# Prompt attention: an order of its own for each engine, and queries turned from the projection's rows without a stage

## The chip, the cores and the metric

The kernel runs on one core of one Trainium2 chip. Its time is the device time of one execution in microseconds (us), the median of several runs. One core has TensorE (the matrix engine), VectorE, ScalarE, GpSimd and SyncE (which here issues DMAs). Each runs its own queue of instructions in order; they meet only at semaphores. In the profile they are PE (and PEld for its weight loads), DVE, ACT, POOL and SP.

## What is computed

One layer of a hybrid decoder, for a prompt of 1024 tokens and for 8 sequences of 8 new tokens. Cut to what matters here:

```python
p = in_proj(rmsnorm(x, norm_pre), w_in)          # q | k,v of three branches | gates | z | gla_* | conv_*
o_nsa = nsa(q, gates, kv_cmp, kv_slc, kv_win) * silu(z)   # 8 query heads x 64, 2 key heads
x = x + rmsnorm(concat(o_nsa, o_gla, o_conv) @ w_out, norm_post)

# nsa, for each block of 128 queries and each of the 4 query heads of a key head:
qs  = q * HEAD_DIM ** -0.5
o_c = softmax(qs @ k_compressed.T, mask) @ v_compressed   # one row per 64 tokens
o_s = softmax(qs @ k_selected.T, causal) @ v_selected     # 16 blocks of 64: for the prompt, all
o_w = softmax(qs @ k_window.T, last 512) @ v_window
o   = gate0 * o_c + gate1 * o_s + gate2 * o_w
```

## The kernel before

The kernel has three stages. `project` norms the input and makes most columns of the projection; `attend_prompt`, which the change rewrites in part, is the prompt's attention; `tail` holds the linear attention, the attention of the new tokens and the output projection. Values are kept nearly at full precision by splitting a tile into a rounded part (`hi`) and the remainder (`lo`), and multiplying both.

The attention works through 32 units: for each of 2 key heads, 8 blocks of 128 queries, each with a selected-branch unit (even numbers, all 1 to 8 key tiles up to the diagonal) and a window unit (odd numbers, at most 5 tiles). For each of a unit's 4 query heads there is a step "scores" (TensorE, line 1084, queries hi and lo against keys, into PSUM banks 0 to 3), a step "least" (VectorE's minimum, L1265) and a step "exp" (ScalarE, L1182). Then, key tile by key tile, "turn" transposes the probabilities of the four heads (TensorE, L1099, into bank 4 or 5), ScalarE copies them rounded (L1190) and VectorE makes the remainder (L1269); "sum" multiplies by the values (L1110, bank 6), and after the last tile ScalarE copies the sums (L1198). "output" turns them back (L1121) and VectorE scales and adds them (L1278 to L1291, tile `scaled`).

Once per block of queries and key head there are also: "query", which turns the queries (TensorE L1056, ScalarE L1170 to q_hi, VectorE L1244 to q_lo), "c_scores" (TensorE L1063 and VectorE L1251 to L1258), "c_exp" (ScalarE L1173, then six VectorE steps from L1298), "c_turn" (TensorE L1127, VectorE L1315) and "c_values" (TensorE L1131, VectorE L1318). These five and "output" share one bank, the spare bank 7: `spare()` makes TensorE wait until VectorE has read the use before. Before "query", VectorE writes the scaled queries twice side by side into the stage `q_st` (`stage_query`, L1207 and L1208), so that the transpose has them on both halves of the partitions; the keys lie there as hi on the first 64 and lo on the last 64.

At the start of each key head come "k_turn", "c_keys" (L1024), "c_rows" (L1031) and "v_stage": the keys and values of this head, turned, compressed and split.

Between all this stands the rest of the projection: 24 items ("rest", L1047) of 8 groups of three products, 192 groups, with the weights' split ("w_split", L1154 and L1234) and the results' way out ("rest_out", L1163, L1240). They use banks 1 and 3, which scores need as well once a unit has more than 4 tiles; so they can only run in the first half of each key head's blocks.

What sets the order: `schedule()` yields one list of steps, with fixed places for everything (`FILL` says how many rest groups go after each head of the first four blocks, `LAG` how far sums stand behind turns). TensorE, ScalarE, VectorE and SyncE all walk this same list, and each takes from it the steps in which it has a part. `place` numbers the uses of the spare bank in list order. `heads_before` and `items_before` find, for each user of banks 1 and 3, whom it has to wait for.

`tail` is ordered in another way: its own `schedule()` inside it is a planner. Each step is given its parts by engine with a duration, and `needs` names what each part waits for. The planner places the steps forward and then backward, and then forward again by the backward places, each engine for itself, and yields a list for each engine.

After the last rest product GpSimd makes the constants of `tail`, and SyncE issues its loads, among them 64 loads of pages (L1388) and the window (L1393).

Of the kernel before, what the change touches and what calls it, by code (L numbers as in the profile page):

```python
# [18 lines left out]
P = 128  # L19
D = 1024  # L20
KD = D // P
# [38 lines left out]
class Order:  # L60
# [19 lines left out]
    def wait(self):  # L80
        at = self.base + self.n
        self.eng.wait_ge(self.sem, at if self.it is None else self.it * self.per + at)

# [531 lines left out]
def attend_prompt(nc, sem, ident, pq, pk, pn, h_hi, h_lo, prob_win, s_cst, w_next, ps, L, z_dram, qk_dram, va_dram, gate_dram, w_in, w_cmp_k, w_cmp_v,  # L615
# [145 lines left out]

    def turn_bank(t):
        return 4 + t % 2
# [18 lines left out]
    with ExitStack() as ctx:  # L782
# [7 lines left out]
        q_st = sb("q_st", [P, NG, 2, HD])  # L790
# [39 lines left out]
        s_qst = sem("q_staged")  # L830
# [14 lines left out]
        with nc.Block() as block:  # L845
# [154 lines left out]
            def _(pe):  # L1000
# [6 lines left out]
                for what, x, y in steps:  # L1007
# [128 lines left out]
            def _(act):  # L1136
                for what, x, y in steps:
# [18 lines left out]
                    elif what == "rest_out":  # L1156
# [44 lines left out]
            def _(dve):  # L1201
                v = Order(dve, v_done)

                def stage_query(x):
                    kv, i = x // NT, x % NT
                    src = pq[:, i, kv * NG * HD:(kv + 1) * NG * HD].rearrange("p (g d) -> p g d", g=NG)
                    nc.vector.tensor_scalar(q_st[:, :, 0, :], src, -SCALE, None, ALU.mult)  # L1207
                    nc.vector.tensor_scalar(q_st[:, :, 1, :], src, -SCALE, None, ALU.mult).then_inc(s_qst, 1)  # L1208

                nc.vector.tensor_scalar(gate, gate, 0.5, 0.5, ALU.mult, ALU.add).then_inc(s_gate, 1)  # L1210
                for what, x, y in steps:
                    if what == "k_stage":
                        if x == 0:
                            stage_query(0)
                    elif what == "v_stage":
# [182 lines left out]
def tail(nc, sem, ident, pq, new, kc, ps, L, z_dram, qk_dram, va_dram, conv_dram, attn_dram, cache_slc_kv, cache_win_kv,  # L1398
# [384 lines left out]
    def sorted_by_need(keys, before):  # L1783
        out, seen = [], set()
        for key in keys:
            todo = [key]
            while todo:
                k = todo[-1]
                wait = [b for b, _ in before[k] if b not in seen]
                if wait:  # L1790
                    todo += wait
                else:
                    todo.pop()
                    if k not in seen:
                        seen.add(k)
                        out.append(k)
        return out

    def schedule():
        HANDOVER, WINDOW = 0.15, 0.3  # L1800
        ENGINES = "PE", "ACT", "DVE", "SP"
        lists = [list(decays()), list(linear()), list(sample_states()), [s for pi in range(PAIRS) for s in pair(pi)], list(project_out()),
                 list(gated(LASTM)), list(split_out())]
        heads, after, before = {}, {}, {}
        for n, steps in enumerate(lists):
            for step in steps:
                done = None
                for eng, cost in parts(step):
                    key = step, eng
                    line = heads.setdefault((n, eng), [])  # L1810
                    before[key] = [((s, e), lag + HANDOVER) for s, e, lag in needs(step, eng)]
                    if done:
                        before[key].append((done, HANDOVER))
                    if line:
                        before[key].append((line[-1][0], 0.0))
                    line.append((key, cost))
                    done = key
        cost = {key: c for line in heads.values() for key, c in line}
        for key in cost:
            for k, lag in before[key]:  # L1820
                after.setdefault(k, []).append((key, lag))

        def place(first, then, rank, window):
            missing = {key: len(first.get(key, [])) for key in cost}
            ready = dict.fromkeys(cost, 0.0)
            open_to = {eng: [key for key in cost if key[1] == eng and not missing[key]] for eng in ENGINES}
            free, at = dict.fromkeys(ENGINES, 0.0), {}
            while len(at) < len(cost):
                begin = lambda key: max(free[key[1]], ready[key])
                soonest, eng = min((min(map(begin, keys)), eng) for eng, keys in open_to.items() if keys)  # L1830
                key = min((key for key in open_to[eng] if begin(key) <= soonest + window), key=rank)
                open_to[eng].remove(key)
                at[key] = free[eng] = begin(key) + cost[key]
                for k, lag in then.get(key, []):
                    ready[k] = max(ready[k], at[key] + lag)
                    missing[k] -= 1
                    if not missing[k]:
                        open_to[k[1]].append(k)
            return at

        left = {}
        for key in reversed(sorted_by_need(cost, before)):
            left[key] = cost[key] + max([lag + left[a] for a, lag in after.get(key, [])], default=0.0)
        forward = place(before, after, lambda key: -left[key], 0.0)
        backward = place(after, before, lambda key: -forward[key], 0.0)
# [884 lines left out]
```

## Time and profile before

| | |
|---|---|
| median of 3 runs | 1014.05 us (1013.36 to 1018.79) |
| the profiled execution | 1020.7 us, of which the span from first to last instruction is 1019.0 us |
| TensorE busy | 935.7 us (92%) |
| VectorE busy | 595.0 us (58%) |
| ScalarE busy | 409.7 us (40%) |
| GpSimd busy | 190.9 us (19%) |
| `project` | about 0 to 285 us of the span |
| `attend_prompt` | about 285 to 720.5 us |
| `tail` | about 720.5 to 1019 us |

"Busy" is the time in which an engine executes; on TensorE the ends are modelled, so two products in a row overlap in the listing. PEclk is the granted clock of TensorE as a share of its full 2.4 GHz; it has two levels, full and half, so a clock of 0.9 over a stretch means a fifth of it at half. "A <- B" behind a wait means that A's engine sat idle until B's instruction released it.

### The profile page before, as it was taken

How to read it: one execution, taken by the hardware profiler on the slowest of the kernel's cores; microseconds unless marked ns; L12 is line 12 of the kernel's file. 1: busy time of each engine (PE TensorE's matmuls, PEld its weight loads, DVE VectorE, ACT ScalarE, POOL GpSimd, SP SyncE). 2: the span in 40 equal slices, each digit the busy share in tenths (PEclk: the TensorE clock that was granted, in tenths of full speed). 3: DMA queues.
4: the chain of work that ended last, by engine and by line, in shares of the span. 5: the costliest groups of instructions: out<-in, count | busy, mean ns of one | idle time of the engine just before them, and what ended most of it. 6: DMA issues, size and time to landing. Idle time of an engine off the chain costs nothing. (4 is left out here: it accounts for less than half of the span.)

```text
span 1019.0 us, 16705 instructions
## 1 busy us (share of the span) xinstructions
PE 935.7 (92%) x5935; PEld 808.9 (79%) x5935; DVE 595.0 (58%) x1428; ACT 409.7 (40%) x916; POOL 190.9 (19%) x178
## 2 busy tenths in 40 slices
PE   5999999998989988999999988999688999999997
PEld 5999999998979887777889867777445666777665
DVE  6531010194444576878555668787567867787653
ACT  6432111111023454666534445667264434434322
POOL 0049599999010000000000230000000000000000
PEclk9999999998999999999999979999688999999999
DMA  7127534534052101000011013300533455452321
GB/s 252 53 97 241 194 114 147 175 118 125 1 169 67 48 16 36 1 1 1 9 43 50 23 39 101 108 1 1 191 91 103 128 166 163 139 160 68 116 89 32
DMA packets 106820, 93.73 MB, mean 92 GB/s; under 512 B 21245, under 2 KB 99954, under 8 KB 104626
## 3 DMA queue, kind: packets, MB, share of 16 engines
q1 hardware_dynamic: 84946, 58.65, 19.1%
q10 hardware_dynamic: 19488, 17.25, 5.6%
q0 software_dynamic: 2304, 16.78, 4.8%
q8 instruction: 47, 0.77, 0.3%
q14 instruction: 35, 0.29, 0.1%
HBM read 78.16 MB, written 18.61 MB: 95 GB/s over the span
## 5 line engine op out<-in xcount | busy, mean ns | idle before, releaser
L592 PE MATMUL ps<-w_hi,h_hi 128*128 128x264 f32 (+5 forms) x432 | 123.9, 287 | 0.2 <-DVE h_lo L464 0.2
L592 PE MATMUL ps<-w_lo,h_hi 128*128 128x264 f32 (+5 forms) x432 | 122.9, 284 | 0.0
L592 PE MATMUL ps<-w_hi,h_lo 128*128 128x264 f32 (+5 forms) x432 | 122.8, 284 | 0.0
L1269 DVE TENSOR_TENSOR pt_lo<-ps,pt_hi 128x512 fp32r<-128x512 f32 x132 | 90.9, 689 | 52.0 <-ACT pt_hi L1190 51.4
L1190 ACT ACTIVATE pt_hi<-ps 128x512 fp32r<-128x512 f32 x132 | 78.6, 597 | 83.2 <-PE ps L1099 82.3
L472 DVE TENSOR_TENSOR w_lo<-w_raw,w_hi 128x1024 fp32r<-128x1024 f32 (+3 forms) x13 | 33.6, 2585 | 128.0 <-ACT w_hi L366 128.0
L1265 DVE TENSOR_REDUCE least<-ps 128x1 f32<-128x640 f32 (+7 forms) x128 | 90.0, 703 | 14.1 <-PE ps L1088 12.9
L313 POOL TENSOR_TENSOR chunk<-chunk 128x1024 f32<-128x1024 f32 (+2 forms) x46 | 82.5, 1793 | 3.6
L592 PEld LDWEIGHTS ps<-w_hi,h_hi 128*128 128x128 f32 (+1 forms) x432 | 79.6, 184 | 0.5 <-issue 0.4
L592 PEld LDWEIGHTS ps<-w_lo,h_hi 128*128 128x128 f32 (+1 forms) x432 | 79.6, 184 | 0.0
L592 PEld LDWEIGHTS ps<-w_hi,h_lo 128*128 128x128 f32 (+1 forms) x432 | 79.3, 184 | 0.0
L1084 PE MATMUL ps<-kT,q_hi 128*128 128x512 f32 (+3 forms) x192 | 74.0, 386 | 2.0 <-DVE stage_b L1240 1.3
L2248 ACT ACTIVATE turned<-ps 128x512 f32<-128x512 f32 (+1 forms) x72 | 39.3, 546 | 80.2 <-PE ps L2011 60.2
L1047 PE MATMUL ps<-h_hi,wr_hi 128*128 128x362 f32 (+1 forms) x192 | 69.5, 362 | 0.5 <-DVE wr_lo L1234 0.5
L592 PE MATMUL ps<-h_hi,w_hi 128*128 128x362 f32 (+1 forms) x192 | 64.4, 335 | 4.8 <-DVE w_lo L472 4.8
L1110 PE MATMUL ps<-pt_hi,vs 128*128 128x512 f32 x132 | 63.6, 482 | 3.6 <-issue 3.4
L1084 PE MATMUL ps<-kT,q_lo 128*128 128x512 f32 (+3 forms) x192 | 65.5, 347 | 0.0
L1047 PE MATMUL ps<-h_lo,wr_hi 128*128 128x362 f32 (+1 forms) x192 | 64.7, 337 | 0.0
L1047 PE MATMUL ps<-h_hi,wr_lo 128*128 128x362 f32 (+1 forms) x192 | 64.7, 337 | 0.0
L592 PE MATMUL ps<-h_hi,w_lo 128*128 128x362 f32 (+1 forms) x192 | 63.9, 333 | 0.0
L592 PE MATMUL ps<-h_lo,w_hi 128*128 128x362 f32 (+1 forms) x192 | 63.9, 333 | 0.0
L1182 ACT ACTIVATE prob_slc<-ps,least 128x128 f32<-128x128 f32 (+7 forms) x64 | 47.4, 741 | 39.7 <-DVE least L1265 39.4
(379 smaller groups left out, 2257.4 us busy)
## 6 DMA issues: line engine op xcount, KB each, us to landing
kv_pages<-in_cache_slc_kv SPq DMA_DIRECT2D x256, 64.0 KB, 1.9
shared<-in_x_prompt SPq DMA_DIRECT2D x8, 512.0 KB, 3.6
w_raw<-in_w_in SPq DMA_DIRECT2D x8, 512.0 KB, 3.9
wr_raw<-in_w_in SPq DMA_DIRECT2D x8, 512.0 KB, 4.0
kv_window<-in_cache_win_kv SPq DMA_DIRECT2D x4, 1024.0 KB, 5.8
wo_raw<-in_w_out SPq DMA_DIRECT2D x8, 512.0 KB, 9.0
out<-in_cache_win_kv SPq DMA_DIRECT2D x1, 4032.0 KB
x_row<-in_x_prompt ACTq DMA_DIRECT2D x7, 512.0 KB, 4.2
```

Source lines behind the costliest of these rows:

```text
L313: g.did(nc.gpsimd.tensor_tensor(out, a, b, ALU.add))
L472: nc.vector.tensor_tensor(half(w_lo, b), raw(b), half(w_hi, b).bitcast(F32), ALU.subtract).then_inc(s_wlo, 1)
L592: mm = nc.tensor.matmul(out, lhs, rhs, start=(k == 0 and i == 0), stop=(k == KD - 1 and i == 2))
L1047: mm = nc.tensor.matmul(ps[:, bank, 0:tn], ww[:, y, :], hh[:, y, t0:t0 + tn], start=(y == 0 and n == 0), stop=(y == KD - 1 and n == 2))
L1084: mm = nc.tensor.matmul(ps[:, bank, 0:n], q[:, i % 2, y * P:(y + 1) * P], kT[:, br, c * P:c * P + n], start=(q is q_hi), stop=(q is q_lo a ...
L1110: mm = nc.tensor.matmul(ps[:, 6, :], vs[:, x % 2, span(x)[0] + y, :, :].rearrange("p a d -> p (a d)"), buf[:, t % PTS, :], start=(y == 0 a ...
L1182: nc.scalar.activation(prob[x % 2][:, y, 0:n], S(y, n), ACT.Exp, scale=-1.0, bias=least[:, h:h + 1], accum_out=rowsum[:, h:h + 1]).then_in ...
L1190: nc.scalar.activation(pt_hi[:, t % PTS, :], ps[:, turn_bank(t), :], ACT.Copy).then_inc(s_pth, 1)
L1265: nc.vector.tensor_reduce(least[:, h:h + 1], S(y, n), AX, ALU.min).then_inc(s_mx, 1)
L1269: nc.vector.tensor_tensor(pt_lo[:, t % PTS, :], ps[:, turn_bank(t), :], pt_hi[:, t % PTS, :].bitcast(F32), ALU.subtract).then_inc(s_ptl, 1)
L2248: nc.scalar.activation(turned[0:rows, m % 3, 0:n], ps[0:rows, TN, 0:n], ACT.Copy).then_inc(s_tbe, 1)
```

## The change

1. `sorted_by_need` and the planner of `tail` become functions of the module, `arrange`. The planner now adds no handover between steps of the same engine, and an extra one after TensorE if asked (0 for `tail`, 0.2 us for the attention).
2. `attend_prompt` describes its steps with durations (`parts`) and needs (`needs`), splits the old list into 8 lists whose inner order is kept, and has `arrange` make an order for each of TensorE, ScalarE and VectorE. SyncE goes on with the old list, and the order of uses of the spare bank stays that of the old list.
3. The stage `q_st` goes. The transposes read 64 columns of `pq` and write 64 partitions; ScalarE copies them twice, with the scale, to the two halves of q_hi; VectorE writes only the first 64 partitions of q_lo, with the scale in the same instruction; the last 64 are zeroed once by GpSimd, so the product of the two remainders is no longer formed.
4. Two waits are added: before the last unit's turns of a key head for the compressed rows of the next one, and before the first plain "rest_out" after a gated one.

```diff
+def arrange(lists, parts, needs, handover, from_pe, window):
+    heads, after, before = {}, {}, {}
+    for n, steps in enumerate(lists):
+        for step in steps:
+            done = None
+            for eng, cost in parts(step):
+                key = step, eng
+                line = heads.setdefault((n, eng), [])
+                before[key] = [((s, e), lag + (0.0 if e == eng else handover + (from_pe if e == "PE" else 0.0)))
+                               for s, e, lag in needs(step, eng)]
+                if done:
+                    before[key].append((done, handover + (from_pe if done[1] == "PE" else 0.0)))
+                if line:
+                    before[key].append((line[-1][0], 0.0))
+                line.append((key, cost))
+                done = key
+    cost = {key: c for line in heads.values() for key, c in line}
+    for key in cost:
+        for k, lag in before[key]:
+            after.setdefault(k, []).append((key, lag))
+
+    def place(first, then, rank, window):
+        missing = {key: len(first.get(key, [])) for key in cost}
+        ready = dict.fromkeys(cost, 0.0)
+        open_to = {eng: [key for key in cost if key[1] == eng and not missing[key]] for eng in ENGINES}
+        free, at = dict.fromkeys(ENGINES, 0.0), {}
+        while len(at) < len(cost):
+            begin = lambda key: max(free[key[1]], ready[key])
+            soonest, eng = min((min(map(begin, keys)), eng) for eng, keys in open_to.items() if keys)
+            key = min((key for key in open_to[eng] if begin(key) <= soonest + window), key=rank)
+            open_to[eng].remove(key)
+            at[key] = free[eng] = begin(key) + cost[key]
+            for k, lag in then.get(key, []):
+                ready[k] = max(ready[k], at[key] + lag)
+                missing[k] -= 1
+                if not missing[k]:
+                    open_to[k[1]].append(k)
+        return at
+
+    left = {}
+    for key in reversed(sorted_by_need(cost, before)):
+        left[key] = cost[key] + max([lag + left[a] for a, lag in after.get(key, [])], default=0.0)
+    forward = place(before, after, lambda key: -left[key], 0.0)
+    backward = place(after, before, lambda key: -forward[key], 0.0)
+    at = place(before, after, lambda key: -backward[key], window)
+    return {eng: [key[0] for key in sorted((k for k in at if k[1] == eng), key=at.get)] for eng in ENGINES}
...
+    FIRST_REST = sum(1 for s in steps[:at["scores", PER_KV // 2, 0]] if s[0] == "rest") // KD
...
+    def parts(step):
+        what, x, y = step
+        n = tiles_of[x] * P if what in ("scores", "least", "exp") else 0
+        if what == "scores":
+            chunks = [min(512, n - c) for c in range(0, n, 512)]
+            edges = 2 if x % 2 == 1 and x % PER_KV // 2 >= WIN // P else 1
+            return (("PE", sum(2 * max(0.112, c * 0.000456) for c in chunks) + 0.09 * edges),)
+        full = {
+            "k_stage": (("DVE", 0.65),) if x == 0 else (),
+            "k_turn": (("PE", 0.45), ("ACT", 0.6), ("DVE", 0.7)),
+            "c_keys": (("PE", 1.8), ("ACT", 0.2), ("DVE", 0.18)),
+            "c_rows": (("PE", 1.8), ("DVE", 0.5)),
+            "v_stage": (("ACT", 0.62), ("DVE", 0.69)),
+            "w_split": (("ACT", 0.41), ("DVE", 0.42)),
+            "rest": (("PE", 0.5),),
+            "rest_out": (("ACT", 0.47), ("DVE", 0.54)) if what == "rest_out" and is_gate(x) else (("ACT", 0.47),),
+            "query": (("PE", 0.45), ("ACT", 1.2), ("DVE", 0.69)),
+            "c_scores": (("PE", 0.9), ("DVE", 0.6)),
+            "c_exp": (("ACT", 0.27), ("DVE", 1.05)),
+            "c_turn": (("PE", 0.11), ("DVE", 0.29)),
+            "c_values": (("PE", 0.3), ("DVE", 0.43)),
+            "least": (("DVE", 0.15 + 0.00105 * n),),
+            "exp": (("ACT", 0.42 + 0.00083 * n),),
+            "turn": (("PE", 0.44), ("ACT", 0.6), ("DVE", 0.69)),
+            "sum": (("PE", 0.47), ("ACT", 0.6)) if what == "sum" and y == tiles_of[x] - 1 else (("PE", 0.47),),
+            "output": (("PE", 0.9), ("DVE", 1.2)),
+        }
+        return full[what]

+    def needs(step, eng):
+        what, x, y = step
+        out = []
+
+        def on(what, x, y, eng, lag=0.0):
+            out.append(((what, x, y), eng, lag))
+
+        def taken(n):
+            on("rest_out", n, 0, "DVE" if is_gate(n) else "ACT")
+
+        if eng == "PE" and (what, x) in spare_before and spare_before[what, x]:
+            k, n = spare_before[what, x]
+            on(spare_step[k], n, 0, "DVE")
+        if what == "k_turn" and eng == "PE":
+            if y >= 2:
+                on("k_turn", x, y - 2, "DVE")
+            elif x > 0 and y == 0:
+                u = PER_KV * x - 2
...
+        elif what == "rest" and y % 2 == 0:
+            if y == 0 and x > 1:
+                taken(x - 2)
+            if x % NCH3 == 0:
+                on("w_split", x // NCH3, y // 2, "DVE")
+            if y == 0 and x == FIRST_REST:
+                on("exp", PER_KV - 1, NG - 1, "ACT")
+        elif what == "rest_out" and eng == "ACT":
+            on("rest", x, KD - 1, "PE")
+            if not is_gate(x) and is_gate(x - 1):
+                on("rest_out", x - 1, 0, "DVE")
+            if x >= 2:
+                on("rest_out", x - 2, 0, "DVE" if is_gate(x - 2) else "ACT", 3.0)
+        elif what == "query" and eng == "PE":
+            on(*(("query", x - 1, 0) if x else ("k_stage", 0, 0)), "DVE")
+            if x % NT == 0:
+                on("c_rows", x // NT, 0, "DVE")
+            if x >= 2:
+                on("scores", (x - 2) // NT * PER_KV + 2 * ((x - 2) % NT) + 1, NG - 1, "PE")
+        elif what == "c_exp" and eng == "ACT":
+            on("c_scores", x, 0, "DVE")
+        elif what == "c_turn" and eng == "PE":
+            on("c_exp", x, 0, "DVE")
...
+        elif what == "scores":
+            h = NG * x + y
+            kv, i = x // PER_KV, x % PER_KV // 2
+            if h >= 2:
+                on("exp", (h - 2) // NG, (h - 2) % NG, "ACT")
+            on("c_scores", kv * NT + i, 0, "PE")
+            if tiles_of[x] > 4:
+                last = (FIRST_REST if kv == 0 else ITEMS) - 1
+                taken(last)
+                taken(last - 1)
...
+                if y == 0:
+                    on("exp", x, NG - 1, "ACT")
+                    if x % PER_KV == PER_KV - 1 and x + 1 < UNITS:
+                        on("c_rows", (x + 1) // PER_KV, 0, "DVE")
+                if t >= 2:
+                    on("turn", *tile(t - 2), "DVE")
...
+    of = lambda *names: [s for s in steps if s[0] in names]
+    order = arrange([of("k_stage", "k_turn", "c_keys", "c_rows"), of("v_stage"), of("scores", "least", "exp"), of("turn"), of("sum"),
+                     of("query", "c_scores", "c_exp", "c_turn", "c_values", "output"), of("rest", "rest_out"),
+                     of("w_split")], parts, needs, 0.15, 0.2, 0.3)
...
-    for what, x, y in steps:
+    for what, x, y in order["PE"]:
...
+                g.did(nc.gpsimd.memset(q_lo[:].bitcast(F32), 0.0))
...
-                        pe.wait_ge(s_qst, x + 1)
                         out = spare(("q", x))
                         for g in range(NG):
-                            mm = nc.tensor.transpose(out[:, g * P:(g + 1) * P],
-                                                     q_st[:, g, :, :].rearrange("p a d -> p (a d)"), ident[:, :])
+                            c = (x // NT * NG + g) * HD
+                            mm = nc.tensor.transpose(out[0:HD, g * P:(g + 1) * P], pq[:, x % NT, c:c + HD], ident[:, :])
...
                             pe.wait_ge(s_exp, NG * (x + 1))
+                            if x % PER_KV == PER_KV - 1 and x + 1 < UNITS:
+                                pe.wait_ge(s_klo, 6 * ((x + 1) // PER_KV) + 6)
...
+                            if is_gate(x - 1):
+                                act.wait_ge(s_rt, x)
...
-                        nc.scalar.activation(q_hi[:, x % 2, :], ps[:, 7, :], ACT.Copy).then_inc(s_qhi, 1)
+                        for rows in (slice(0, HD), slice(HD, P)):
+                            mm = nc.scalar.activation(q_hi[rows, x % 2, :], ps[0:HD, 7, :], ACT.Copy, scale=-SCALE)
+                        mm.then_inc(s_qhi, 1)
...
-                def stage_query(x):
-                    kv, i = x // NT, x % NT
-                    src = pq[:, i, kv * NG * HD:(kv + 1) * NG * HD].rearrange("p (g d) -> p g d", g=NG)
-                    nc.vector.tensor_scalar(q_st[:, :, 0, :], src, -SCALE, None, ALU.mult)
-                    nc.vector.tensor_scalar(q_st[:, :, 1, :], src, -SCALE, None, ALU.mult).then_inc(s_qst, 1)
-
...
-                        nc.vector.tensor_tensor(q_lo[:, x % 2, :], ps[:, 7, :],
-                                                q_hi[:, x % 2, :].bitcast(F32), ALU.subtract
-                                                ).then_inc(s_spr, 1)
-                        if x + 1 < NKV * NT:
-                            stage_query(x + 1)
+                        nc.vector.scalar_tensor_tensor(q_lo[0:HD, x % 2, :], ps[0:HD, 7, :], -SCALE,
+                                                       q_hi[0:HD, x % 2, :].bitcast(F32), ALU.mult, ALU.subtract
+                                                       ).then_inc(s_spr, 1)
...
-    order = schedule()
+    order = arrange([list(decays()), list(linear()), list(sample_states()), [s for pi in range(PAIRS) for s in pair(pi)], list(project_out()), list(gated(LASTM)), list(split_out())], parts, needs, 0.15, 0.0, 0.3)
```

## Rows read from the trace of the kernel before

**Rows 1.** Stretches: start:end, length, busy us of five engines, PEclk, DMA share, GB/s.
```profile
285.00:420.00 135.00, 122.68 (x783) 114.40 (x781) 81.38 (x220) 59.81 (x159) 4.20 (x17) 0.96 0.20 62
420.00:500.00 80.00, 74.33 (x462) 62.66 (x462) 62.74 (x123) 50.94 (x102) 0.00 (x0) 0.98 0.00 1
500.00:640.00 140.00, 126.91 (x799) 116.77 (x798) 84.57 (x222) 62.93 (x162) 15.30 (x57) 0.94 0.18 51
640.00:720.50 80.50, 74.28 (x464) 61.85 (x462) 61.82 (x121) 50.64 (x100) 0.00 (x0) 0.98 0.10 29
720.50:1019.00 298.50, 270.47 (x1486) 187.84 (x1486) 204.30 (x625) 115.32 (x266) 0.00 (x0) 0.93 0.41 124
760.00:960.00 200.00, 191.48 (x1145) 136.57 (x1145) 151.53 (x478) 83.33 (x193) 0.00 (x0) 0.97 0.46 134
840.00:960.00 120.00, 117.96 (x693) 86.05 (x691) 89.84 (x275) 50.09 (x117) 0.00 (x0) 1.00 0.46 136
```
**Rows 2.** Waits of TensorE, 285 to 720.5 us: us in total, times, longest.
```profile
PE ps L1127 <- DVE scaled L1283: 8.5, 6, 1.8
PE ps L1063 <- DVE q_lo L1244: 5.3, 8, 0.9
PE ps L1131 <- DVE c_pT L1315: 3.6, 6, 0.8
...
PE ps L1056 <- DVE scaled L1283: 3.2, 4, 1.1
...
PE ps L1131 <- DVE scaled L1283: 2.6, 3, 0.9
```
**Rows 3.** Timeline, 388 to 400 us: start, us, engine, line, what.
```profile
391.18 0.22 DVE L1298 TENSOR_TENSOR c_s<-c_s,c_mask 128x64 f32<-128x64 f32 x1 [0.88 <-ACT c_s L1173]
...
393.91 0.42 DVE L1283 TENSOR_TENSOR scaled<-ps,factor 128x256 f32<-128x256 f32 x1
...
394.39 0.33 PE L1127 MATMUL ps<-ident,c_p 128*128 128x128 f32 x1 [1.75 <-DVE scaled L1283]
```
**Rows 4.** Groups by shape, 285 to 720.5 us: count, busy us, mean ns, idle before.
```profile
L1244 DVE TENSOR_TENSOR q_lo<-ps,q_hi 128x512 fp32r<-128x512 f32 x16 | 11.1, 692 | 17.8 <-ACT q_hi L1170 17.8
L1170 ACT ACTIVATE q_hi<-ps 128x512 fp32r<-128x512 f32 x16 | 9.5, 595 | 16.4 <-PE ps L1056 16.4
L1240 DVE SCALAR_TENSOR_TENSOR stage_b<-stage_b,ps 128x362 f32<-128x362 f32 x12 | 6.4, 531 | 6.5 <-ACT stage_b L1163 6.4
L1208 DVE TENSOR_SCALAR q_st<-pq 128x256 f32<-128x256 f32 x16 | 5.1, 319 | 0.0
L1147 ACT ACTIVATE kT<-ps 64x512 fp32r<-64x512 f32 x8 | 4.7, 589 | 10.1 <-PE ps L1017 10.1
L1207 DVE TENSOR_SCALAR q_st<-pq 128x256 f32<-128x256 f32 x16 | 4.6, 288 | 0.0
```
**Rows 5.** TensorE in two stretches of 5 us: length, busy, PEclk, DMA, GB/s.
```profile
390.00:395.00 5.00, 2.92 (x19) 1.00 0.33 97
395.00:400.00 5.00, 5.00 (x22) 0.66 0.00 0
```
**Rows 6.** Timeline of TensorE, around the compressed values of the second key head.
```profile
507.21 0.32 PE L1047 MATMUL ps<-h_lo,wr_hi 128*128 128x362 f32 x1
...
509.07 1.98 PE L1031 MATMUL ps<-pk,wv 128*128 128x64 f32 x16
...
511.11 0.50 PE L1047 MATMUL ps<-h_hi,wr_lo 128*128 128x364 f32 x1
```
**Rows 7.** Timeline of SyncE's queue: the last load for the last stage.
```profile
650.06 0.43 SPq L1393 DMA_DIRECT2D kv_window<-in_cache_win_kv  x1
```
**Rows 8.** GpSimd's zeroing of 512 columns (groups); its last constant and the user (timeline).
```profile
L942 POOL MEMSET q_heads<- 128x512 f32 x1 | 0.6, 552 | 290.8 <-PE ps L1047 290.8
...
289.43 0.11 POOL L938 MEMSET c_stat<- 128x12 f32 x1
...
294.48 1.84 PE L1024 MATMUL ps<-wk,pk 128*128 128x2 f32 x16
```

More of the change, by code:

```diff
@@ L82, in wait, with sorted_by_need @@
         self.eng.wait_ge(self.sem, at if self.it is None else self.it * self.per + at)
+ENGINES = "PE", "ACT", "DVE", "SP"
+def sorted_by_need(keys, before):
+    out, seen = [], set()
+    for key in keys:
+        todo = [key]
+        while todo:
+            k = todo[-1]
+            wait = [b for b, _ in before[k] if b not in seen]
+            if wait:
+                todo += wait
+            else:
+                todo.pop()
+                if k not in seen:
+                    seen.add(k)
+                    out.append(k)
+    return out
@@ L760, in attend_prompt @@
     place = {x: n for n, x in enumerate(uses)}
+    FIRST_REST = sum(1 for s in steps[:at["scores", PER_KV // 2, 0]] if s[0] == "rest") // KD
+    spare_before = {}
+    for n, (k, x) in enumerate(uses):
+        what = {"q": "query", "cs": "c_scores", "ct": "c_turn", "co": "c_values", "z": "output"}[k]
+        spare_before[what, x] = uses[n - 1] if n else None
+    spare_step = {"q": "query", "cs": "c_scores", "ct": "c_turn", "co": "c_values", "z": "output"}
+    is_gate = lambda n: REST[n // NCH3][0] == "gate"
@@ new lines, in needs @@
+    def needs(step, eng):
[13 more added lines that the diff above has]
+                u = PER_KV * x - 2
+                on("turn", u, tiles_of[u] - 1, "DVE")
+                on("scores", u + 1, NG - 1, "PE")
+            elif x > 0:
+                u = PER_KV * x - 2
+                on("sum", u, tiles_of[u] - 1, "ACT")
+        elif what == "c_keys" and eng == "PE":
+            on("k_turn", x, 2, "DVE")
+        elif what == "c_rows" and eng == "PE":
+            on("k_turn", x, 3, "DVE")
+            if x > 0:
+                on("c_values", x * NT - 1, 0, "PE")
+        elif what == "v_stage" and eng == "ACT" and x > 0:
+            u = PER_KV * x - 2 + y
+            on("sum", u, tiles_of[u] - 1, "PE")
+        elif what == "w_split" and eng == "ACT" and x > 0:
+            on("rest", NCH3 * x - 1, 2 * y + 1, "PE")
+            if y == 0:
+                on("w_split", x - 1, KD // 2 - 1, "DVE", 6.0)
+        elif what == "rest" and y % 2 == 0:
[21 more added lines that the diff above has]
+            on("c_exp", x, 0, "DVE")
+        elif what == "c_values" and eng == "PE":
+            on("c_turn", x, 0, "DVE")
+        elif what == "output" and eng == "PE":
+            on("sum", x, tiles_of[x] - 1, "ACT")
+        elif what == "scores":
[8 more added lines that the diff above has]
+                taken(last - 1)
+        elif what == "least":
+            on("scores", x, y, "PE")
+        elif what == "exp":
+            on("least", x, y, "DVE")
+            if x >= 2:
+                on("turn", x - 2, tiles_of[x - 2] - 1, "PE")
+        elif what in ("turn", "sum"):
+            t = first_tile[x] + y
+            tile = lambda t: next((u, t - first_tile[u]) for u in range(UNITS) if first_tile[u] <= t < first_tile[u + 1])
+            if what == "turn" and eng == "PE":
+                if y == 0:
+                    on("exp", x, NG - 1, "ACT")
[3 more added lines that the diff above has]
+                    on("turn", *tile(t - 2), "DVE")
+            elif what == "turn" and eng == "ACT" and t >= PTS:
+                on("sum", *tile(t - PTS), "PE")
+            elif what == "sum" and eng == "PE":
+                on("turn", x, y, "DVE")
+                if y == 0:
+                    on("v_stage", x // PER_KV, x % 2, "DVE")
+                    if x > 0:
+                        on("sum", x - 1, tiles_of[x - 1] - 1, "ACT")
+            elif what == "sum" and x > 0:
+                on("output", x - 1, 0, "PE")
+        return out
@@ L789, in attend_prompt @@
         stage = sb("stage_b", [P, 2, 364])
-        q_st = sb("q_st", [P, NG, 2, HD])
         kT = sb("kT", [P, 2, SEQ], F32R)
@@ L1005, in spare @@
                     return ps[:, 7, :]
-                for what, x, y in steps:
+                for what, x, y in order["PE"]:
                     if what == "k_turn":
@@ L1136, in _ @@
             def _(act):
-                for what, x, y in steps:
+                for what, x, y in order["ACT"]:
                     if what == "v_stage":
@@ L1202, in _ @@
                 v = Order(dve, v_done)
-                def stage_query(x):
-                    kv, i = x // NT, x % NT
-                    src = pq[:, i, kv * NG * HD:(kv + 1) * NG * HD].rearrange("p (g d) -> p g d", g=NG)
-                    nc.vector.tensor_scalar(q_st[:, :, 0, :], src, -SCALE, None, ALU.mult)
-                    nc.vector.tensor_scalar(q_st[:, :, 1, :], src, -SCALE, None, ALU.mult).then_inc(s_qst, 1)
-                nc.vector.tensor_scalar(gate, gate, 0.5, 0.5, ALU.mult, ALU.add).then_inc(s_gate, 1)
[L1211 to L1215, printed above, removed]
+                nc.vector.tensor_scalar(gate, gate, 0.5, 0.5, ALU.mult, ALU.add).then_inc(s_gate, 1)
+                for what, x, y in order["DVE"]:
+                    if what == "v_stage":
                         c = x * HD + BR[y][0] + P
@@ L1781, in needs @@
         return out
[L1783 to L1845, printed above, removed]
-        at = place(before, after, lambda key: -backward[key], WINDOW)
-        return {eng: [key[0] for key in sorted((k for k in at if k[1] == eng), key=at.get)] for eng in ENGINES}
```

1 line of the change is left out of this document (removed).

## The prediction

> **What bounds the kernel now.** I read the busy time by stretches first. The change works in the prompt attention, which lies from 285 to 720.5 us of the span, so I cut that into four: 285 to 420 and 500 to 640, where the remaining projection ("rest") is at hand as filler, and 420 to 500 and 640 to 720.5, where it is used up [rows 1]. TensorE is busy 122.7 of 135, 74.3 of 80, 126.9 of 140 and 74.3 of 80.5 us: it is the bound in all four and idle for 12.3 + 5.7 + 13.1 + 6.2 = 37.3 us. VectorE, the next, has 62.7 of 80 where it is fullest. The granted clock is 0.96, 0.98, 0.94, 0.98; with the two levels 2.4 and 1.2 GHz that is 10.8 + 3.2 + 16.8 + 3.2 = 34 us at half clock (length x (1 - clock) x 2), and half of these, 17 us, are lost if TensorE had work all along. So 54 us are at most to be had by order alone.
>
> Second view, TensorE's waits inside the attention [rows 2]. The five rows shown all concern the spare bank, PSUM bank 7, which queries, compressed scores, turned probabilities, compressed values and outputs take in turn: 8.5 + 5.3 + 3.6 + 3.2 + 2.6 = 23.2 us, 62% of the idle time. Third view, the timeline of one such wait [rows 3]: VectorE multiplies the compressed mask at 391.18, goes through the other small steps of c_exp, then a score minimum and a split of turned probabilities, and only at 393.91 frees the bank by reading `scaled`; the turn of compressed probabilities, next in TensorE's queue, starts at 394.39 after 1.75 us of idle. Nothing there is a shortage of throughput. All engines follow one list written by hand, so the step that TensorE needs stands behind steps that nobody needs yet, and what TensorE could do meanwhile stands behind the one that waits.
>
> **Part 1: an order of its own for each engine.** It adds and removes no TensorE, VectorE or ScalarE instruction. It lets TensorE slip rest groups and other heads' scores under such waits, and lets VectorE read the bank first. What an order from this planner yields can be read from the last stage, which has it already: from 760 to 960 us TensorE is busy 191.5 of 200 (4.3% idle), from 840 to 960 it is 118.0 of 120 (1.7%) [rows 1].
> - With filler (275 us, 25.4 us idle): at 1.7% idle 4.5 us would stay, at 4.3% 11 us; saved 14 to 21. I take 17, between the two, since 192 groups of filler, 3 products of some 362 columns each, are there to put into the holes. The lower bound is 0: the hand-made order stays as good.
> - Without filler (160.5 us, 11.9 us idle): at 4.3% 6.6 us stay, saved 5; at 1.7% saved 9; at worst 0. I take 5. VectorE allows it: with TensorE never idle in 420 to 500 it would be busy 62.7 of 74.3 us.
> - The clock: 17 us lost now. In 390 to 395 TensorE is busy 2.92 of 5 us and in the next 5 us the clock is 0.66 [rows 5]; most of the drops follow such holes, and from 840 to 960, with few holes, the clock is 1.00 [rows 1]. But one drop has no hole before it: the compressed keys and values are made with products of 2 and 64 columns, one after another to 511 us, and the products behind take 0.50 us in place of 0.32 [rows 6]. These steps stay, once per key head, and so may their drops. I take 6 of 17; bounds 0 and 13 (17 less one drop of about 3.4 us at half clock, 1.7 us, for each key head).
>
> The clock term can be weighed against the Trainium skill, "TensorE: Matmul & The Clock Gate", section "A second HAM failure mode: psum-queue depth-cycling": it tells of a kernel in which short idles between groups of matmuls, bank by bank, were enough to make the clock swing. The trace agrees at 390 to 400 us [rows 5] and shows at 511 us a fall without any idle [rows 6]. By the rule alone the whole clock loss would go with the holes and the sum would be 11 us lower; by the row at 511 alone nothing of it would.
>
> **Part 2: the queries.** Gone are two VectorE multiplies per query, 288 and 319 ns, x16 = 9.7 us of VectorE [rows 4]. The four transposes read `pq` with 64 columns as the stationary side and still stream 128: no change on TensorE. ScalarE writes q_hi in two copies of 64 x 512 instead of one of 128 x 512; a copy of 64 x 512 takes 589 ns against 595 [rows 4], so the number of partitions saves nothing and each query costs 0.59 us more: 16 x 0.59 = 9.4 us. ScalarE is busy 50.9 of 80 us in the fullest stretch [rows 1], which is the cover; without it the 9.4 us come on the path (rival 2). q_lo becomes one scaled subtraction of 64 x 512. The form was not seen at this size; the like of it takes 531 ns for 362 columns, the plain subtraction of 512 columns 692 [rows 4]. Scaled by columns the first would be 0.75 us, so -0.1 to +0.1 us x16; I take 0. The 9.7 us of VectorE are no bound's time; that they are gone helps the waits counted in part 1 and gets no term of its own (at most 2 us beside it).
>
> **Part 3: the zeroing of q_lo** stands ahead of GpSimd's other constants. It is 1024 columns; 512 took 552 ns, so about 1.1 us [rows 8]. The constants were ready at 289.4 and their user, the compressed keys, started at 294.5 [rows 8]: covered. The planner doesn't know this wait, and may put that step up to 5 us earlier; then 0 to 1.5 us are lost once. I take 0. **The new wait** of the last unit's turns for the compressed rows of the next key head keeps the banks that both use (4 and 6) apart; that order holds in the list of before as well. Queued behind it are TensorE's sums of that unit: 0. The other new wait, ScalarE's before the first plain rest_out, comes once; exps stand behind it, for at most one VectorE pass of 0.53 us [rows 4]: 0.
>
> **Part 4: the last stage** is planned by the same rules, but without a handover between steps of one engine. Its order may shift in places; 28 us of its 298.5 are idle [rows 1]. I take 0, with -3 and +3 as bounds.
>
> **SyncE** keeps the old list. Its weight loads and stores follow steps whose relative order hardly changes. After the last rest product it loads pages and window for the last stage, the last one issued at 650.06 us [rows 7]; 70 us lie between that and 720.5, so rest groups moved later by some 20 us cost nothing.
>
> **Sum:** 17 + 5 + 6 = 28 us. The profiled execution took 1020.7 us (span 1019.0), so it would be 992.7; that execution lies 6.6 us above the median of the three timed runs, 1014.05, and the same 28 us from the median give 986.
>
> **Rivals.**
> 1. The spare bank stays the bound. The order of its uses is carried over from the old list, and each use must be read before the next is written. Against it: at 391 us the delay was other work on VectorE, not the chain itself. For it: 23.2 of 37.3 us hang on this bank [rows 2] and each query holds it 0.59 us longer. If half of the 23.2 us stay, 0.6 of the other idle time goes and the clock gives nothing back, (37.3 - 23.2) x 0.6 + 11.6 - 9.4 = 10.7 us are saved: 1003.5 to 1009.
> 2. Slower. The chain query transposes, ScalarE's copies, VectorE's q_lo, compressed scores becomes 0.59 us longer 16 times, and in a fixed order TensorE stands before the compressed scores with nothing placed in front of them. TensorE waits there for q_lo already, 8 times, 5.3 us [rows 2]. If the planner's fixed durations are off (at half clock TensorE's steps take double) and its order waits as often as the old one, the 9.4 us come on top: 1023.5. It decides once the rearrangement saves less than 9.4 us.
> 3. The orders come out much as before, because the buffers (two probability tiles, three turned, two score banks) already fix them: 1009 to 1019. Against it: VectorE had the freed bank waiting behind work that no buffer forced.
> 4. More than forecast: holes shrink to the best stretch's 1.7% and the clock keeps full: 21 + 9 + 13 = 43 us, 971. It is the end of my own case.
>
> **Chances.** Forecast 0.69 (own range 971 to 1003), rival 1 0.13, rival 3 0.07, rival 2 0.11. Range 969 to 1012: it leaves out the slower case and most of the unchanged one. Measurement of this kernel tells 0.5%, about 5 us, from no change: faster 0.82 (forecast and rival 1), within 0.07, slower 0.11.
>
> **What would show it.** Right: TensorE's idle time in the attention falls from 37 us to some 15, the waits of the turned compressed probabilities for `scaled` nearly vanish, rest products are spread up to the fifth tile row of each key head instead of ending at 580 us, half-clock time falls below 22 us, the last stage keeps 298 us. Rival 1: waits of bank 7 above 12 us. Rival 2: waits for q_lo above 10 us. My forecast is wrong if TensorE's waits go and its busy time in the attention grows by as much (the clock), or if the last stage changes by over 5 us.

## The result and the profile after

The changed kernel takes 955.98 us (median of 4 runs, 953.67 to 958.68) against 1014.61 for the kernel before: ratio 0.9416, interval 0.9375 to 0.9457, 58.6 us less. The forecast was 986 (range 969 to 1012); the result lies below the range. The direction and the main mechanism (orders of their own take away TensorE's waits at the spare bank) held, the forecast gain of 28 us was half of what came. The profiled execution took 957.8 us (span 956.0); the profiled execution of before lies 6 us above its median, so the spans differ by 63 us, and the medians are the measure.

The busy time by stretches; the columns are those of [rows 1]. The attention now lies from 285 to 663 us.

```profile
285.00:663.00 378.00, 374.32 (x2504) 346.01 (x2504) 282.78 (x652) 236.74 (x538) 20.91 (x78) 0.99 0.16 48
285.00:420.00 135.00, 133.75 (x887) 126.56 (x887) 93.36 (x231) 78.37 (x192) 5.66 (x21) 0.97 0.21 64
420.00:500.00 80.00, 79.89 (x545) 73.42 (x545) 63.36 (x138) 52.11 (x112) 0.00 (x0) 0.98 0.05 13
500.00:600.00 100.00, 99.73 (x672) 93.06 (x671) 72.14 (x177) 62.44 (x150) 15.26 (x57) 1.00 0.12 36
600.00:663.00 63.00, 60.94 (x406) 52.98 (x404) 53.91 (x110) 43.81 (x87) 0.00 (x0) 1.00 0.27 79
```

In the first row: TensorE is busy 374.3 of 378 us, where [rows 1] add up to 398.2 of 435.5. So not only has its idle time shrunk from 37.3 to 3.7 us; the same instructions are also listed with 23.9 us less. That second part is what the forecast did not have.

TensorE's waits, 285 to 680 us, the columns of [rows 2] (the rows of lines above L1540 belong to the last stage and are left out):

```profile
PE ps L1227 <- PEq L303: 1.7, 1, 1.7
...
PE ps L1332 <- ACT oT L1413: 0.8, 1, 0.8
...
PE ps L1257 <- DVE wr_lo L1440: 0.7, 1, 0.7
PE ps L1310 <- DVE pt_lo L1473: 0.5, 2, 0.2
...
PE ps L1293 <- ACT prob_slc L1397: 0.4, 2, 0.2
...
PE ps L1321 <- issue: 0.3, 1, 0.3
```

Every wait for the spare bank in [rows 2] is gone: the turned compressed probabilities (now L1338), the compressed scores (L1272), the compressed values (L1342) and the queries (L1266) don't appear. The timeline of the fifth block of the first key head answers to [rows 3]:

```profile
386.50 0.21 DVE L1502 TENSOR_TENSOR c_s<-c_s,c_mask 128x64 f32<-128x64 f32 x1
...
387.50 1.00 PE L1332 MATMUL ps<-ident,oT 128*128 128x64 f32 x8
387.62 0.82 DVE L1469 TENSOR_REDUCE least<-ps 128x1 f32<-128x640 f32 x1
...
388.76 0.42 DVE L1487 TENSOR_TENSOR scaled<-ps,factor 128x256 f32<-128x256 f32 x1
388.86 0.39 PE L1293 MATMUL ps<-kT,q_hi 128*128 128x512 f32 x1
...
389.89 0.39 PE L1321 MATMUL ps<-pt_lo,vs 128*128 128x512 f32 x1
390.12 0.27 PE L1338 MATMUL ps<-ident,c_p 128*128 128x128 f32 x1
```

VectorE still has a score minimum between, but the remainder of the turned probabilities no longer stands ahead of `scaled`, which comes 0.3 us after the output's last product. And TensorE doesn't stand before the bank: between the output at 387.50 and the turn at 390.12 it has placed two sums and one head's scores. No rest product is among them: the first key head's last one started at 381.15 us.

The queries, by shape, answer to [rows 4]:

```profile
L1384 ACT ACTIVATE q_hi<-ps 64x512 fp32r<-64x512 f32 x32 | 18.8, 589 | 10.0 <-PE ps L1266 9.8
L1450 DVE SCALAR_TENSOR_TENSOR q_lo<-ps,q_hi 64x512 fp32r<-64x512 f32 x16 | 10.9, 679 | 10.9 <-ACT q_hi L1384 10.9
```

Two copies of 589 ns are as forecast; the scaled subtraction takes 679 ns, a little less than the plain one of [rows 4].

### The profile page after: what moved, and what is told of

Read it like the earlier page. It is cut to its first block and busy times, and to the rows that moved or that the text cites. A ratio compares the mean times of both kernels' runs of the same rounds, so it can differ in the third digit from the quotient of the medians.

```text
span 956.0 us, 16677 instructions
## 1 busy us (share of the span) xinstructions
PE 906.1 (95%) x5935; PEld 796.0 (83%) x5935; DVE 588.0 (62%) x1396; ACT 421.0 (44%) x932; POOL 191.8 (20%) x179
## 5 line engine op out<-in xcount | busy, mean ns | idle before, releaser
L1257 PE MATMUL ps<-h_hi,wr_hi 128*128 128x362 f32 (+1 forms) x192 | 72.1, 376 | 0.7 <-DVE wr_lo L1440 0.7
L1293 PE MATMUL ps<-kT,q_hi 128*128 128x512 f32 (+3 forms) x192 | 69.8, 364 | 0.4 <-ACT prob_slc L1397 0.4
L391 POOL TENSOR_TENSOR chunk<-chunk,wb 128x2048 f32<-128x2048 f32 x16 | 58.6, 3660 | 15.5 <-DMA chunk<-in_cache_cmp_kv,rows 15.1
L1321 PE MATMUL ps<-pt_hi,vs 128*128 128x512 f32 x132 | 60.0, 455 | 0.3 <-issue 0.3
```

The lines of the kernel that those rows point to most:

```text
L391: g.did(nc.gpsimd.tensor_tensor(x, x, wb[:, :, l0:l0 + CHT].rearrange("p k t -> p t k").unsqueeze(3).to_broadcast([P, CHT, 2, ROW]), ALU.m ...
L1257: mm = nc.tensor.matmul(ps[:, bank, 0:tn], ww[:, y, :], hh[:, y, t0:t0 + tn], start=(y == 0 and n == 0), stop=(y == KD - 1 and n == 2))
L1293: mm = nc.tensor.matmul(ps[:, bank, 0:n], q[:, i % 2, y * P:(y + 1) * P], kT[:, br, c * P:c * P + n], start=(q is q_hi), stop=(q is q_lo a ...
L1321: mm = nc.tensor.matmul(ps[:, 6, :], vs[:, x % 2, span(x)[0] + y, :, :].rearrange("p a d -> p (a d)"), buf[:, t % PTS, :], start=(y == 0 a ...
```

## Where 58 us come from

A reader's first question is how more can be saved than the 54 us that the prediction called the most that could be had. Three rows of the kernel before show it; they lie just ahead of the wait in [rows 3]:

```profile
390.28 0.33 PE L1047 MATMUL ps<-h_hi,wr_lo 128*128 128x364 f32 x1
390.45 0.33 PE L1047 MATMUL ps<-h_lo,wr_hi 128*128 128x364 f32 x1
391.10 0.47 PE L1110 MATMUL ps<-pt_hi,vs 128*128 128x512 f32 x1 [0.32 <-issue]
```

In a stream a product starts 0.17 us after the one before it (390.28, 390.45), though each is listed with 0.33 us. The next could have started at 390.62; it starts at 391.10. The hole costs 0.48 us, of which the listing calls 0.32 idle and counts the other 0.16 as the last product's own time. So each hole costs its listed idle time and some 0.17 us more. I took each start-to-start time in the attention and held it against the usual one of its kind and shape at full clock (the 30th percentile over both kernels); a hole is a start later than the listed end of the product before:

| traced kernel | attention, first to last start | holes | idle listed | lost at the holes in all | excess at half clock (time in it) |
|---|---|---|---|---|---|
| before | 435.5 | 73 | 37.1 | 49.9 | 15.9 (34.1) |
| before, second execution | 431.7 | 73 | 37.1 | 49.9 | 11.7 (23.9) |
| after | 377.0 | 10 | 2.9 | 4.7 | 4.7 (10.2) |
| after, second execution | 372.9 | 10 | 3.0 | 4.7 | 0.0 (0.0) |

From the first execution of before to the first of after: 34.2 us of listed idle, 11.0 us more at the same holes, 11.2 us of clock, 2 us elsewhere, 58.5 in all. The second pair gives 34.1, 11.1, 11.7 and 2, 58.8. Held against the medians' 58.6 us, the attention carries the whole change. A third execution of the same attention, in the run with the last stage planned as before (below), has 10 holes, 2.9 us idle and no time at half clock.

## The experiments

All but the last start from the changed kernel. "Ratio" is to the kernel before, run on the same chip, with its 95% interval.

**The old order with the new queries.**

```diff
-    order = arrange([of("k_stage", "k_turn", "c_keys", "c_rows"), ...], parts, needs, 0.15, 0.2, 0.3)
+    order = dict.fromkeys(("PE", "ACT", "DVE"), steps)
```

> The changed kernel with the attention's engines walking the one hand-made list again (queries without a stage kept, last stage as changed). Theory: the orders carry the gain, so this stands near the kernel before: TensorE idle in the attention 34 to 42 us, 12 us more hidden in its busy time, half clock about 34 us; ScalarE's second copy adds up to 5 us to the waits for q_lo; the last stage's 5 us may be kept: 1008 to 1020 us. Rival (the shorter VectorE work of the queries carries part of the gain): 1003 us or less.

Measured 1022.24 us, ratio 1.0047 (1.0018 to 1.0077). In the trace 71 holes, 42.6 us idle, 34.1 us at half clock. TensorE's waits for q_lo, then for `scaled`:

```profile
PE ps L1270 <- DVE q_lo L1448: 12.4, 14, 1.5
PE ps L1336 <- DVE scaled L1485: 8.6, 6, 1.8
```

The first is 5.3 us in [rows 2]. The query change, with the two added waits and the new plan of the last stage beside it, costs some 5 us under the old order (2 to 8 by the interval) and buys nothing; the orders carry the gain. The upper end of the expectation was 2 us low.

**The new orders with the staged queries.** `q_st`, its two VectorE multiplies, its wait and the one full copy are back; the planner has 0.6 us for ScalarE and 1.27 for VectorE.

> The changed kernel with the staged queries of before (two VectorE multiplies per query, one ScalarE copy), the planner told so. Theory: orders alone keep the gain, 954 to 962 us, because VectorE gets 9.7 us more and ScalarE 9.4 us less, both under TensorE. Rival (VectorE is nearly the bound in the denser attention, 63.4 of 80 us busy, so each VectorE step counts): 966 us or more.

Measured 954.47 us, ratio 0.9397 (0.9366 to 0.9427): the same as with the new queries. Under the new orders the form of the query makes no difference that can be told, as the theory had it.

**One shared list.**

```diff
+    shared = ...  # all steps by the planner's time of their first part, needs respected
+    order = dict.fromkeys(("PE", "ACT", "DVE"), shared)
```

> The changed kernel, but TensorE, ScalarE and VectorE walk one common list, made from the planner's times (a step stands where its first part is placed). Theory (own orders matter: a step's VectorE part must not stand where its TensorE part does): a third to two thirds of the attention's gain is lost, 975 to 998 us, with TensorE waiting again for VectorE's reads of the spare bank. Rival (a better list is all that it takes): 962 us or less.

Measured 1001.73 us, ratio 0.9836 (0.9795 to 0.9878), 4 us beyond the expected band; 54 holes, 31.7 us idle. A better list alone brings 17 us, over a quarter of the gain. The waits are of another kind now:

```profile
PE ps L1320 <- ACT prob_slc L1424: 7.9, 10, 1.2
PE ps L1348 <- issue: 7.6, 7, 2.0
PE ps L1320 <- ACT prob_win L1424: 3.4, 7, 0.7
PE ps L1337 <- ACT prob_slc L1424: 3.3, 4, 2.3
```

TensorE waits for the exps (before scores at L1320, before turns at L1337) and before sums (L1348), no longer mainly for the spare bank. My reading, argued and not shown: in one list a step's later parts stand where its first part does, too early for some and too late for others. Another single list might do better than this one.

**Only TensorE free, and only ScalarE and VectorE free.** The planner keeps the named engines to their order in the old list:

```diff
+    for eng in fixed:
+        keys = [(step, eng) for step in chain if (step, eng) in cost]
+        for a, b in zip(keys, keys[1:]):
+            before[b].append((a, 0.0))
```

> The changed kernel, with TensorE's order free and ScalarE and VectorE each held to their order in the old list (the planner knows it). Theory (both halves are needed: TensorE must slip work under the waits, and VectorE must read the bank early): about half of the attention's 58 us gain, 975 to 995 us; TensorE's holes 25 to 45 in number, idle 10 to 20 us. Rival (TensorE's queue alone was the trouble): 962 us or less.

> The changed kernel, with ScalarE's and VectorE's orders free and TensorE held to its order in the old list. Theory (the same): 980 to 1005 us, since TensorE has nothing to slip under a wait, but VectorE frees the spare bank sooner: its waits for the bank's readers fall from 23 us to under 15. Rival (the whole gain was VectorE reading the bank late, as the one wait shown at 391 us): 962 us or less.

Measured 1000.64 us, ratio 0.9856 (0.9811 to 0.99), and 1000.22 us, ratio 0.986 (0.9813 to 0.9906). The first lies 6 us beyond its band, with 64 holes and 25.0 us idle where 25 to 45 and 10 to 20 were expected; the second lies in its band, with 52 holes and 30.9 us idle. TensorE's waits, of the first and then of the second kernel:

```profile
PE ps L1276 <- DVE q_lo L1454: 9.0, 9, 1.6
PE ps L1314 <- DVE pt_lo L1477: 4.7, 11, 0.7
PE ps L1346 <- DVE c_pT L1523: 2.7, 5, 0.8
```

```profile
PE ps L1276 <- DVE q_lo L1454: 10.2, 13, 1.5
PE ps L1342 <- DVE scaled L1491: 4.4, 6, 1.2
```

With TensorE free the waits for `scaled` are gone from the top of the list; with the others free they stay, at half (4.4 us for L1342, 8.5 in [rows 2]). But the forecast of the second run, that the waits for the bank's readers fall from 23 us to under 15, missed: the same five rows have 10.2 + 4.4 + 2.5 + 2.3 + 2.2 = 21.6 us. The waits for `scaled` and `c_pT` fell from 17.9 to 11.4, and those for q_lo rose from 5.3 to 10.2, as they also did under the old order with the new queries (12.4). Against the kernel with the old order and new queries (1022.2) each half gains 22 us and both together 66 (by the ratios, 19 and 64). So a third of those 66 us comes only with both. I read it so, which the runs don't show step by step: TensorE can slip more work under a wait if the engines that prepare it have it ready, and their being early is of more use if TensorE can take it.

**No filler.**

```diff
-            if tiles_of[x] > 4:
+            if tiles_of[x] > 4 or x % PER_KV == 0:
```

> The changed kernel, but all rest products of a key head must be out before its first scores, so that nothing of them can fill holes later. Theory (the gain in the first blocks of each key head hangs on the filler, since there the chain of the spare bank is longer than TensorE's other work): 975 to 1000 us, idle TensorE in the first four blocks of each key head 15 to 35 us, more half clock. Rival (other heads' scores and turns fill as well): 962 us or less.

Measured 975.65 us, ratio 0.9588 (0.9541 to 0.9634); 31 holes, 14.4 us idle. The low end of the theory, and less idle than the 15 to 35 us expected in the first four blocks alone: the filler is worth 20 of the 59 us, two thirds come without it. 4.6 us of the loss are this kernel's own, one wait of TensorE for the next weights (the changed kernel has 0.7 us at that line), since the rest products now run in one piece:

```profile
PE ps L1257 <- DVE wr_lo L1440: 5.3, 2, 4.6
```

**Flat durations.**

```diff
-        return full[what]
+        return tuple((eng, 0.6) for eng, _ in full[what])
```

Scores, which are worked out ahead of that table, get 0.6 too.

> The changed kernel with every duration in the planner set to 0.6 us, needs and handovers unchanged. Theory (the freedom of separate orders gives most, the durations the rest; a rest group of 0.5 us and a chain step of 0.9 us confused costs some holes): 962 to 985 us. Rival (orders only help if the durations are right, since a fixed order blocks at the first mistake): 1000 us or more.

Measured 990.52 us, ratio 0.9754 (0.9712 to 0.9796); 38 holes, 22.1 us idle. Between theory and rival, nearer to the theory: with needs and handovers alone 25 us are gained, the right durations bring the other 34.

**The last stage planned as before.**

```diff
-                               (0.0 if e == eng else handover ...)
+                               (0.15 if e == eng else handover ...)   # for the last stage only
```

(In short; in the kernel the value is a new argument of `arrange`, 0 for the attention.)

> The changed kernel with the last stage planned as before (0.15 us of handover also between steps of one engine); the attention is untouched. Theory (the 5 us that the last stage lost, 298.5 to 293 us, come from its own new order): about 961 us, last stage 297 to 299 us. Rival (they come from the clock or from where the stage starts, not from the order): 954 to 957 us, last stage 292 to 294 us.

Measured 956.67 us, ratio 0.9429 (0.9404 to 0.9454): the same. From the attention's last TensorE start to the end the trace has 294.0 us, with the old plan. The rival held and the theory (961 us, 297 to 299) fell: the last stage's new order gains nothing that can be told.

**Compressed values apart from the compressed keys, and the changed kernel again.**

```diff
+            on("rest", *((14, 5) if x else (1, 3)), "PE")   # a need of c_rows
```

> The changed kernel, with one more need in the planner: the compressed values (products of 64 columns) come after 2 or 3 rest groups that follow the compressed keys (products of 2 columns), in place of right behind them. In the changed kernel the clock fell to half right behind these two, for 3.4 us, at 296.9 and at 481.2 us. Theory (the fall belongs to 3.6 us of such small products in a row): neither fall is there, 3 us less: 951 to 954 us where the changed kernel has 956. Rival (the falls have another cause, or the delay of the compressed values costs as much): 955 to 960 us.

> As the one before, with the staged queries of the kernel before. Theory (stage or no stage is the same under TensorE): within 2 us of it, 950 to 955 us. Rival (in the densest stretches ScalarE's second copy still reaches TensorE): 3 us or more under it.

> The changed kernel once more, on the same chip as the two others, to compare with: 954 to 958 us; the last stage 293 us again if its 5 us are the kernel's, up to 299 if they were one execution's.

Measured 953.98 us (0.9406, 0.937 to 0.9443), 955.32 us (0.9415, 0.9379 to 0.9451) and, for the changed kernel again, 955.51 us (0.9426, 0.9385 to 0.9466). No difference can be told. The falls of the clock are not in the traces of the first two, but neither are they in the second execution of the changed kernel, nor in the execution with the last stage's old plan, whose attention is the same. TensorE from 292 to 297 and 297 to 302 us, in its first execution:

```profile
292.00:297.00 5.00, 5.00 (x43) 0.99 1.03 325
297.00:302.00 5.00, 5.00 (x24) 0.67 0.59 147
```

and in its second:

```profile
292.00:297.00 5.00, 5.00 (x41) 1.00 1.00 329
297.00:302.00 5.00, 5.00 (x34) 1.00 0.59 154
```

So the same small products are followed by a fall in one execution and by none in another, and whether the spacing helps stays open. It is not a version worth keeping on this evidence.

**The kernel before, again.** Unchanged.

> The kernel before once more, unchanged, for its trace. Open is the last stage: 298.9 us in the trace of before, 294 to 297 in the others, with either plan of that stage. Theory (it is one execution's, by its clock): here 294 to 297 us, and the attention again 435 us with some 73 holes, 37 us idle and 34 us at half clock. Rival (the change makes the last stage shorter): 298 to 300 us.

One execution of 1014.03 us. From the attention's last TensorE start to the end: 296.0 us, where the first trace of before had 298.9 and the changed kernel's two have 293.7 and 296.7. The attention is as before (table above), only with 10 us less at half clock. So most of the 5 us between the first two traces was one execution's: over all other runs this stretch lies between 291.3 and 296.7 us, with either plan of the last stage. Whether 1 or 2 us of it are the kernel's can't be told.

## Why the prediction was wrong

- **What bounds it**: right. TensorE was the bound, and its waits at the spare bank, set by VectorE's place in the list, went with the orders. But "54 us are at most to be had" was false: it took the listed idle time as all that a hole costs. The 73 holes cost 12.8 us beside it, of which 11 are gone.
- **Part 1, idle time**: the step that failed most. Taken were 17 + 5 = 22 us, measured 34. I read the last stage, 1.7 to 4.3% idle, as what such a planner reaches, but that stage has other chains; the attention came to 0.8% (2.9 of 377 us). The split by filler was misread as well. The last rest products of the two key heads start at 400.4 and 579.9 us in the kernel before, not at 420 and 640, and at 381.2 and 564.0 us in the changed one. TensorE behind them, before and then after (columns as in [rows 5]):

```profile
401.00:498.00 97.00, 89.30 (x562) 0.98 0.01 3
580.50:720.30 139.80, 125.24 (x759) 0.94 0.16 47
```

```profile
381.50:469.80 88.30, 87.99 (x598) 1.00 0.01 3
564.40:662.50 98.10, 96.16 (x647) 1.00 0.23 67
```

  So 22.3 of the 37.3 us idle lay where no filler was left, not 11.9, and only 2.3 stayed there: 20 us saved without filler, where 5 were forecast, and 14 with it, where 17 were. What fills the holes there is other scores, turns and sums.
- **Part 1, clock**: taken 6, measured 11 to 12. I let falls behind small products stay for certain; they come in some executions only. Over all the traces the time at half clock in the attention goes with the holes: 24 to 34 us with 71 to 73 holes, 14 to 17 with 31 to 64, 0 to 10 with 8 to 10. The rule that I weighed there, that short idles between groups of matmuls make the clock swing (the Trainium skill, "TensorE: Matmul & The Clock Gate", section "A second HAM failure mode: psum-queue depth-cycling"), would have had the sum nearer: without the holes one execution had 10.2 and another 0 us at half clock, against 34.1 and 23.9 in the two of before. The term itself came out midway between my 6 and the rule's 17.
- **Missing term**: 11 us, the starts behind the holes. 22 + 6 = 28 became 34 + 11 + 11 + 2.
- **Part 2**: its price of 9.4 us for ScalarE is right as busy time; on the path it is 5 us under the old order and 0 under the new ones. The mechanism of rival 2 was real (waits for q_lo of 12.4 us under the old order), its condition (orders that wait as often as the old one) was not met.
- **Part 3**: right. The zeroing took 0.96 us; the constants were ready at 291.3, the compressed keys started at 293.4. **Part 4 and SyncE**: right, 0; the window's load went out at 631.5 us, 31 us ahead of the last stage, a smaller margin than the 70 of [rows 7].
- **Rival 1** fell: the order of uses of the bank was kept and its waits vanished all the same. **Rival 3** fell. Of the signs named, one misled: the last stage changed by just over 5 us between the first two traces, and the later ones show that as mostly one execution's. **Rival 4**, 43 us, was set as the end of my case because its ends were the last stage's share and the listed idle time: both too tight.

## What to carry to other kernels

When a dense engine waits often in short pieces, count the holes and add to the listed idle time what each hides in the product before it (here 0.17 us), then the half-clock time. A shared list is a hidden tie between engines: free the feeding engines and the fed one together, each alone brought a third here (22 of 66 us), and one better shared list 17 of 59. And give a planner measured durations; with equal ones it brought 25 us in place of 59.

## What was not expected of the hardware

The listed length of a product (0.33 us for 364 columns) is twice its start-to-start time in a stream (0.17), so a TensorE listed as 91% busy in the attention (398.2 of 435.5 us) was at 83% of the pace of its own usual start-to-start times at full clock (360.9 of 435.5 us); the changed kernel's second execution reached 97% (360.9 of 372.9). The granted clock fell to half behind the same sequence of small products in one execution of the same kernel and not in another. A ScalarE copy of 64 partitions costs as much as one of 128 (589 and 595 ns), which the prediction had from [rows 4].
